# Order of the wide and narrow products inside an up projection's tile: eight wide, then eight narrow

## The reference, cut to what matters

```
def swiglu_ffn(x, norm_g, w_in, w_out):                  # twice, hidden width 2816
    gate, up = jnp.split(rmsnorm(x, norm_g) @ w_in, 2, axis=-1)
    return (jax.nn.silu(gate) * up) @ w_out
...
    u = jax.nn.relu(rmsnorm_2(x, ln2[l]) @ w_ff1[l])     # once, hidden width 4096
    x = x + (u * u) @ w_ff2[l]
```

## Time and profile before

| | us |
|---|---|
| median of three runs | 1037.17 |
| lowest and highest | 1036.7, 1037.73 |
| the profiled execution, its own time | 1036.92 |
| its span, from the first instruction to the last | 1035.2 |

### The profile page before, as it was taken

The page is one execution under the profiler, slowest core; times in us unless marked ns, Lnnn a source line. Parts: engine busy times, 40 slices in busy tenths (PEclk is TensorE's granted clock), DMA queues, the critical chain, the costliest instruction groups (busy, mean ns, idle before and its releaser), DMA issues.

```text
span 1035.2 us, 15770 instructions
## 1 busy us (share of the span) xinstructions
PE 1017.5 (98%) x6374; PEld 872.3 (84%) x6374; DVE 714.2 (69%) x1123; ACT 540.3 (52%) x846; POOL 91.7 (9%) x143
## 2 busy tenths in 40 slices
PE   8998999999999999999999999999999999999997
PEld 8976888888889957888888889999779988888885
DVE  5998866666667696657766678748756457656654
ACT  6336545455454596555545553545655445444442
POOL 4000390000010131000000021000000000000000
PEclk9999999999999999999999999999999999999999
DMA  9983656666636404755766646554245345665631
GB/s 267 250 203 103 200 176 194 203 198 179 200 82 212 156 1 123 224 163 169 219 202 183 202 133 216 173 163 164 82 163 178 107 148 177 191 204 176 201 125 41
DMA packets 189327, 174.71 MB, mean 169 GB/s; under 512 B 13028, under 2 KB 164708, under 8 KB 189255
## 3 DMA queue, kind: packets, MB, share of 16 engines
q1 hardware_dynamic: 187280, 169.67, 54.2%
q10 hardware_dynamic: 1398, 3.12, 0.9%
q0 software_dynamic: 576, 0.92, 0.3%
HBM read 171.76 MB, written 1.93 MB: 168 GB/s over the span
## 4 chain that ended last, share of the span: by engine, by line
PE 88%; DVE 6%; ACT 4%; issue 1%; POOL 0%; DMA 0%; ACTq 0%; POOLq 0%; DVEq 0%
PE bank L1982 15%; PE bank L1984 15%; PE bank L1983 15%; PE bank L2050 11%; PE bank L2054 11%; PE bank L2053 5%; PE bank L2051 5%; DVE split_lo L1167 2%; PE bank L2234 2%; DVE xn L1184 1%; ACT xn L740 1%; PE bank L2434 1%; DVE v L1685 1%; PE bank L2006 1%; PE bank L2650 1%
## 5 line engine op out<-in xcount | busy, mean ns | idle before, releaser
L1167 DVE TENSOR_TENSOR split_lo<-raw,split_hi 128x2048 fp32r<-128x2048 f32 (+1 forms) x159 | 356.5, 2247 | 140.7 <-ACT split_hi L700 140.4
L700 ACT ACTIVATE split_hi<-raw 128x2048 fp32r<-128x2048 f32 (+1 forms) x159 | 297.5, 1874 | 88.7 <-PE bank L1984 82.2
L2050 PE MATMUL bank<-xn,split_hi 128*128 128x512 f32 x480 | 190.5, 397 | 0.7 <-DVE xn L1184 0.7
L2054 PE MATMUL bank<-xn,split_hi 128*128 128x512 f32 x480 | 189.9, 396 | 0.0
L1982 PE MATMUL bank<-xn,split_hi 128*128 128x256 f32 (+2 forms) x496 | 143.1, 289 | 2.3 <-DVE xn L1184 1.6
L1983 PE MATMUL bank<-xn,split_hi 128*128 128x256 f32 (+2 forms) x496 | 140.2, 283 | 0.0
L1984 PE MATMUL bank<-xn,split_lo 128*128 128x256 f32 (+2 forms) x496 | 140.1, 283 | 0.0
L2053 PE MATMUL bank<-xn,split_lo 128*128 128x256 f32 x480 | 133.6, 278 | 0.0
L2051 PE MATMUL bank<-xn,split_lo 128*128 128x256 f32 x480 | 133.2, 277 | 0.0
L1982 PE MATMUL bank<-split_hi,ffa_hi 128*128 128x512 f32 x320 | 124.9, 390 | 0.0
L1984 PE MATMUL bank<-split_hi,ffa_lo 128*128 128x512 f32 x320 | 124.5, 389 | 0.0
(11 more groups left out here) (344 smaller groups left out, 1342.2 us busy)
## 6 DMA issues: line engine op xcount, KB each, us to landing
raw<-in_ffn_w_in SPq DMA_DIRECT2D x88, 512.0 KB, 5.1
raw<-in_w_ff SPq DMA_DIRECT2D x32, 1024.0 KB, 5.5
raw<-in_ffn_w_out SPq DMA_DIRECT2D x22, 1024.0 KB, 5.0
raw<-in_w_in SPq DMA_DIRECT2D x14, 1024.0 KB, 5.2
raw<-in_w_xkv SPq DMA_DIRECT2D x8, 1024.0 KB, 5.4
raw<-in_a_pw_w SPq DMA_DIRECT2D x12, 512.0 KB, 7.3
raw<-in_a_pw_w SPq DMA_DIRECT2D x4, 1024.0 KB, 9.7
raw<-in_b_w_in SPq DMA_DIRECT2D x4, 1024.0 KB, 5.9
```

The source lines that it names most:

```text
L700: nc.scalar.activation(split_slot[m % SPLITS][0][:, 0:n], raw[c % RAWS][:, 0:n], ACT.Copy).then_inc(split_hi, 1)
L1167: return nc.vector.tensor_tensor(dst, src, hi.bitcast(F32), ALU.subtract)
L2050: mm(whole, hi, xn_both[:, :, kt, :], start=kt == 0, stop=False)
L2054: x = mm(whole, hi, xn_both[:, :, kt, :], start=False, stop=kt == KT - 1)
```

## The change

`both_halves` issues all wide products of the slices that it is called with, then all narrow products of the same slices. Number, operands, accumulation and target of the matmuls are the same, and so are the semaphores; the waits on `xn_ready` (with `ready`) now stand between the wide products alone. The mark that starts the accumulation stays on the wide product kt = 0, the mark that ends it moves from the wide to the narrow product kt = 7.

```
             def both_halves(b, w, c0, kts=range(KT), ready=None):
 
                 whole = bank[b][:, :].rearrange("p (e t) -> p e t", e=2)
+                hi, lo = part(w, ALL, ALL, slice(c0, c0 + P))
                 for kt in kts:
                     if ready is not None and kt % 2 == 0:
                         te.wait_ge(xn_ready, ready + kt // 2 + 1)
-                    hi, lo = part(w, ALL, kt, slice(c0, c0 + P))
-                    if kt % 2 == 0:
-                        mm(whole, hi, xn_both[:, :, kt, :], start=kt == 0, stop=False)
-                        x = mm(bank[b][:, 0:S], lo, xn[0][:, kt, :], start=False, stop=False)
-                    else:
-                        mm(bank[b][:, 0:S], lo, xn[0][:, kt, :], start=False, stop=False)
-                        x = mm(whole, hi, xn_both[:, :, kt, :], start=False, stop=kt == KT - 1)
+                    mm(whole, hi[:, kt, :], xn_both[:, :, kt, :], start=kt == 0, stop=False)
+                for kt in kts:
+                    x = mm(bank[b][:, 0:S], lo[:, kt, :], xn[0][:, kt, :], start=False, stop=kt == KT - 1)
                 return x
```

## The result

The median of 20 runs after is 1038.89 us, beside 1037.55 us for 20 runs of the kernel before: ratio 1.0014, interval [1.0008, 1.002]. That is 1.3 to 1.5 us slower, less than the 2.07 us named as the line for "no difference", but the interval excludes no change. The forecast was 0.7 us faster, and the median lies 0.3 us above the upper end of its range, 1038.6. The profiled execution took 1038.94 us, its span is 1037.2.

The account below looks back on a forecast made before the run. TensorE's queue alone was taken as the bound: -1.4 us from the plain tiles and +0.7 from the first pairs make -0.7 us, median 1036.5 us, range 1035.3 to 1038.6 us.

Parts of the forecast that it names:

- no difference: Whole kernel: a change within 0.2% of the time, 2.07 us, counts as the same; chance of same 0.83.
- TensorE alone sets the pace: Up projections: TensorE's queue is the only bound, at clock 1.00; time between two starts goes straight into the total.
- A tile before takes 2.786 us: Plain pairs, 114 tiles: 2.786 us before, 2.774 after at 226.7 and 120.0 ns per product; 1.4 us less.
- At the changes from one kind to the other something is carried over: Switches between wide and narrow products: plus and minus 0.01 us, which cancel.
- The first pairs cost 0.22 us each, 0.7 in all: First pair of each of three stages: waits on xn_ready make tile 1 start 0.22 us later; 0.7 us in all.
- Nothing else moves: Rest of the kernel: no wait, transfer or instruction of another engine goes or comes; first_tile, used and copies stay.
- two pairs of ffn0 in 11.10 us: Sign in the profile after: two plain pairs of ffn0 take 11.10 us instead of 11.14.
- the order makes no difference in the plain tiles: Rival, plain tiles: they cost the same in either order, only the first pairs count; +0.7 us, 1037.9; chance 0.23.
- The slower rival: Plain tiles: narrow products rise to 120 ns, wide ones stay at 233; +5.0 us with first pairs, 1042.2; chance 0.09.
- The base: Whole kernel: starting median of 1037.17 us, to which the forecast change of -0.7 us was added.

Follow-up runs that it names:

- the run with the plain pairs alone: Wide-then-narrow order only in the 57 plain pairs, old order in the three first pairs, against the kernel before: 1038.41 us, ratio 1.0011.
- the run with the first pairs alone: Wide-then-narrow order only in the three first pairs, old order in the other 57, against the kernel before: 1038.2 us, ratio 1.0007.
- the run with 32: In ffn0 and ffn1, 32 wide products of two pairs, then their 32 narrow ones; old order in first pairs; against kernel before: 1076.5 us, ratio 1.0376.

## Why the prediction was wrong, step by step

- *TensorE alone sets the pace, at full clock:* right; stage by stage the difference of the traces is the difference of the times.
- *A tile before takes 2.786 us; settled runs go at 226.7 and 120.0 ns, also for the two-part input and for lo weights alone:* right, both to the nanosecond.
- *"At the changes from one kind to the other something is carried over: ... they cancel":* this step failed. I read it from the three starts behind a narrow pair, and at +0.01 us. Behind eight narrow products five distances are affected and 27 ns are carried, of which the head of the narrow run gives back 7. So the term was 20 ns a tile instead of none. With the 12 ns that the settled paces do save, a tile got about 7 ns dearer (27 ns in a period of four), the plain pairs came to +0.7 us (the run with the plain pairs alone) instead of -1.4, and the sum changed its sign. The row with the right size stood in the trace of before, at 633.91.
- *The first pairs cost 0.22 us each, 0.7 in all:* right. kt 6 and tile 1 started where the text put them (tile 1 forecast at 121.47; measured 122.04 less the 0.57 us of the later start), and the run with the first pairs alone gave +0.68.
- *Nothing else moves:* right; no wait on splits or banks came or went. But the sign "two pairs of ffn0 in 11.10 us" failed with the third step, 11.14 and 11.15 measured, and the stretch leaves out the switch into the down projection.
- *Rivals:* "the order makes no difference in the plain tiles" gave +0.7 us and was nearer than the forecast, for no reason that held. The slower rival had the sign but not the mechanism: the wide products do settle at 226.7, though with their disturbed starts they average 229.2 ns in a period, close to the 229.8 from which that rival was to decide.
- *The base:* the sum stood on a median of three runs, 1037.17; that of 20 is 1037.55. Without that 0.4 us the measured median would have lain at 1038.5, just inside the range. The range also says that it takes in 0.5 us of scatter, but only the low end has it; with it the high end would be 1039.1.

## What to carry to other kernels

When an edit reorders a queue that never runs dry, price the transitions with rows that have the same run length ahead of them, not only the settled paces: here the settled paces promised 1.4 us and the transitions took 2.1. Before work is moved from between two waits, compare what is left there with the distance between the two arrivals. And a coarser order delivers its first results later: four tiles to a switch were to save 20 ns of transitions a group and cost 1.6 us, since the next splits stood in ScalarE's queue behind the copies of these results.

## What the runs showed of the hardware that I had not expected

- The distance between starts of back-to-back matmuls (each with its own load of 128 x 128) has a settled value, 226.7 ns for 512 columns and 120.0 for 256, and a disturbed one. Behind eight or more matmuls of 256 columns those of 512 settle after five distances (233, 236, 228, 233, 230), as they do after the restart behind a wait (335, 231, 236, 228, 233, 230, in the run with 32); alternating one by one they never do (233 to 241).
- The total isn't monotonous in the run length: 260, 53, 93, 153, 80 and 40 ns above the settled paces a period with runs of 1, 2, mixed 3 and 2, 4, 8 and 16.
- A narrower stationary operand isn't always cheaper: with 48 columns instead of 128 the products of 256 columns fell from 120 to 116 ns, and those of 512 rose from 227 to between 233 and 239 (the tile behind a down projection), though each load was recorded with 0.12 us instead of 0.19.
